# Sixteen experts in fourteen units: experts ordered by token count on the chip, shared units in column groups, four homes for weights

## What is computed

```
def moe_ffn(h, w_router, b_router, w1, w3, w2):
    s = sigmoid(h @ w_router); sb = s + b_router          # 16 experts in 4 groups
    gsel = argmax over groups of the sum of the group's top two sb
    idx = the two best experts inside that group; wsel = s[idx] / sum(s[idx])
    hid = silu(h @ w1[e]) * (h @ w3[e])                   # 1024 -> 256, for the chosen e
    return sum over the two chosen e of wsel * (hid @ w2[e])   # 256 -> 1024
```

## Time and profile before

| | us |
|---|---|
| median of 3 runs | 1189.07 (1189.02 to 1189.97) |
| the profiled execution's own time | 1190.82 |
| its span, first to last instruction | 1189.2 |
| PE busy | 1121.5 (94%) |
| DVE busy | 536.3 (45%) |
| ACT busy | 282.8 (24%) |
| POOL busy | 208.8 (18%) |
| mean granted TensorE clock | 0.992 |

### The profile page before, as it was taken

The page is one execution under the profiler, slowest core; times in us unless marked ns, Lnnn a source line. Parts: engine busy times, 40 slices in busy tenths (PEclk is TensorE's granted clock), DMA queues, the critical chain, the costliest instruction groups (busy, mean ns, idle before and its releaser), DMA issues.

```text
span 1189.2 us, 13631 instructions
## 1 busy us (share of the span) xinstructions
PE 1121.5 (94%) x4356; PEld 604.3 (51%) x4356; DVE 536.3 (45%) x1275; ACT 282.8 (24%) x653; POOL 208.8 (18%) x288
## 2 busy tenths in 40 slices
PE   5999999998999999999799999989899879999995
PEld 3556766554444454444355676745544435444442
DVE  1146543874237433433441545477623644333326
ACT  2121222663011211111141112156601111111111
POOL 5026101010115100000463410000112230000022
PEclk9999999999999999999999999999999999999998
DMA  9577822893207899998865941178300589999954
GB/s 350 209 245 289 315 109 92 349 370 145 107 26 279 323 386 366 368 367 302 322 231 154 388 149 36 43 293 337 107 18 0 189 343 354 359 373 371 358 176 196
DMA packets 63318, 291.17 MB, mean 245 GB/s; under 512 B 9504, under 2 KB 10672, under 8 KB 47328
## 3 DMA queue, kind: packets, MB, share of 16 engines
q1 hardware_dynamic: 33344, 190.87, 42.8%
q0 software_dynamic: 22720, 78.75, 18.6%
q10 hardware_dynamic: 7200, 20.87, 4.4%
HBM read 240.06 MB, written 56.98 MB: 250 GB/s over the span
## 4 chain that ended last, share of the span: by engine, by line
PE 84%; DVE 6%; DMA 4%; issue 2%; ACT 2%; POOL 1%; SPq 0%; ACTq 0%; POOLq 0%; DVEq 0%
PE ps L1235 13%; PE ps L1536 12%; PE ps L1715 9%; PE ps L1693 9%; PE ps L1696 9%; PE ps L1170 3%; PE ps L1163 3%; PE ps L1470 2%; PE ps L1501 2%; PE ps L1481 2%; PE ps L1146 2%; PE ps L1749 2%; DMA expert_in<-arena,pos_i 2%; PE ps L1145 2%; PE ps L1101 2%
## 5 line engine op out<-in xcount | busy, mean ns | idle before, releaser
L1235 PE MATMUL ps<-arena 128*128 128x320 f32 x560 | 156.6, 432 | 0.0
L1536 PE MATMUL ps<-arena 128*128 128x512 f32 x320 | 140.4, 594 | 2.4 <-issue 2.4
L1235 PEld LDWEIGHTS ps<-arena 128*128 128x128 f32 x560 | 105.0, 190 | 42.6 <-issue 1.0
L1715 PE MATMUL ps<-arena 128*128 128x512 f32 x256 | 115.4, 594 | 3.7 <-issue 3.7
L1693 PE MATMUL ps<-arena 128*128 128x512 f32 x256 | 117.2, 601 | 1.3 <-DVE arena L2791 1.3
L1696 PE MATMUL ps<-arena 128*128 128x512 f32 x256 | 115.1, 592 | 0.0
L2791 DVE COPY arena<-ps 128x512 f32<-128x512 f32 x32 | 22.1, 691 | 203.3 <-PE ps L1676 203.3
L1536 PEld LDWEIGHTS ps<-arena 128*128 128x128 f32 x320 | 59.5, 190 | 74.6 <-issue 74.6
L1693 PEld LDWEIGHTS ps<-arena 128*128 128x128 f32 x256 | 48.9, 192 | 62.5 <-issue 60.4
L1696 PEld LDWEIGHTS ps<-arena 128*128 128x128 f32 x256 | 48.6, 190 | 61.2 <-issue 61.2
L1715 PEld LDWEIGHTS ps<-arena 128*128 128x128 f32 x256 | 46.1, 190 | 50.5 <-issue 50.5
(11 more groups left out here) (332 smaller groups left out, 1652.2 us busy)
## 6 DMA issues: line engine op xcount, KB each, us to landing
arena<-in_w SPq DMA_DIRECT2D x96, 1024.0 KB, 9.3
arena<-in_w_ada SPq DMA_DIRECT2D x40, 1024.0 KB, 6.8
expert_in<-arena POOLq DMA_DIRECT2D x2, 8192.0 KB, 33.4
expert_out<-arena ACTq DMA_DIRECT2D x30, 512.0 KB, 8.1
arena<-expert_in POOLq DMA_DIRECT2D x28, 512.0 KB, 9.7
arena<-in_w_t SPq DMA_DIRECT2D x10, 1024.0 KB, 10.6
arena<-in_w_ada_c SPq DMA_DIRECT2D x8, 1024.0 KB, 13.2
arena<-in_w_out SPq DMA_DIRECT2D x8, 1024.0 KB, 6.1
```

The costliest lines, as they stand in the source:

```text
L1235: ins = mm(out[:, 0:HALF], lhs[:, k, :], rhs[:, k, :], start=(first and k == 0), stop=(last and k == 3), skip_group_check=True)
L1536: ins = mm(out[:, n * 512:(n + 1) * 512], yT[:, k, t * P:(t + 1) * P], w[k // 2][:, k % 2, n * 512:(n + 1) * 512], start=(k == 0), stop=(k ...
L1715: ins = mm(out[:, n * 512:(n + 1) * 512], hidT[:, f, :], w[:, f, n * 512:(n + 1) * 512], start=(f == 0), stop=(f == 1))
```

## The change

Nothing before the router changes. After the counts of tokens per expert are known, DVE orders experts 2 to 15 by count (larger count first) with pairwise comparisons of 14 by 14 and gives each a role: roles 2 to 9 are the eight with the fewest tokens ("low"), roles 10 to 15 the others; experts 0 and 1 keep roles 0 and 1. `roles_i` holds the expert of each role; each engine that needs it reads it with `value_load`. A low role has room for 96 rows a round, the others for 128. If more than six of the fourteen have over 96 rows, two rounds are run.

Four low roles share three units: each unit takes 96 rows of one role and 32 rows of the fourth. Two full units, six shared ones and six full ones make fourteen. In a shared unit every matmul is written as four, each over 32 columns of the token block, which land in 32 rows of the output; three use one expert's weights, one the other's. The loops over units are written out instead of hardware loops. There are four homes for weights; the two new ones lie where h2 was, so they are free only after the scatter. The slot rows in `expert_out` are numbered by role. An extra transfer of 1 MB of zeros at the beginning fills the 32 rows of low roles that no store writes.

```diff
+LOW_CAP = 96
+LOW_ROLES = 8
+def expert_units():
+    units = [[(0, 0, P, 0)], [(1, 0, P, 0)]]
+    for low in (2, 6):
+        units += [[(low + i, 0, LOW_CAP, 0), (low + 3, LOW_CAP, P - LOW_CAP, (P - LOW_CAP) * i)] for i in range(3)]
+    return units + [[(role, 0, P, 0)] for role in range(LAST_LOW, NE)]
+PLACE_OF = {0: 0, 1: 1, 2: 2, 5: 3, 3: 0, 4: 1, 6: 2, 9: 0, 7: 1, 8: 3, 10: 2, 11: 1, 12: 3, 13: 2, 14: 0, 15: 1}
+LOAD_ORDER = list(PLACE_OF)
+WEIGHTS_ORDER = sorted([(load, role) for role in LOAD_ORDER[2:-2] for load in ("up", "down")],
+                       key=lambda x: 2 * FIRST_UNIT[x[1]] + 3 * (x[0] == "down"))
...
+        up_at = [at_ring + SLOT, at_ring + 3 * SLOT, at_h + 2 * SLOT, at_h]
+        down_at = [at_ring, at_ring + 5 * SLOT, at_h + 4 * SLOT, at_up]
...
# SP
-                    load_up(2, 0, 0)
...
+                    wait(sp, roles_ready.sem, roles_ready.at(l, 1))
+                    filled(sp, l, "tokens0")
+                    wait(sp, scattered.sem, scattered.at(l, 16 * 2 * TT))
...
+                        for load, role in WEIGHTS_ORDER:
+                            e = sp.value_load(roles_i[0:1, role:role + 1], min_val=0, max_val=NE - 1)
+                            free = used_by(base, role)
+                            (load_up if load == "up" else load_down)(e, PLACE_OF[role], base + 2 if free is None else free)
...
# POOL
+                    pool.dma_start(y_d.rearrange("(e p) d -> p e d", p=P)[LOW_CAP:P, FIRST_LOW:LAST_LOW],
+                                   zeros[LOW_CAP:P, :].unsqueeze(1).broadcast_to((P - LOW_CAP, LOW_ROLES, D))).then_inc(spare_zeroed, 16)
...
+                        def load(u):
+                            b = u % 2
+                            wait(pool, hs_in[b], turn * of_round(ROWS_IN, b) + before_unit(ROWS_IN, u))
+                            wait(pool, hsT_full, base + u + 1)
+                            for role, lo, n, skipped in EXPERT_UNITS[u]:
+                                e = pool.value_load(roles_i[0:1, role:role + 1], min_val=0, max_val=NE - 1)
+                                src = slots_in(e, r) if n == P else some_slots_in(e, r, skipped, n)
+                                pool.dma_start(hs[lo:lo + n, b, :], src).then_inc(hs_in[b], 16)
...
# PE
+                def columns_of_unit(u):
+                    parts = EXPERT_UNITS[u]
+                    if len(parts) == 1:
+                        return [(0, P, parts[0][0])]
+                    return [(lo + i, 32, role) for role, lo, n, _ in parts for i in range(0, n, 32)]
...
+                    for k in range(KD):
+                        if k == 4:
+                            pe.wait_ge(hsT_high, base + u + 1)
+                        for lo, n, role in columns_of_unit(u):
+                            ins = mm(out[lo:lo + n, :], hsT[b][:, k, lo:lo + n], w[role][:, k, :], start=(k == 0), stop=(k == KD - 1),
+                                     skip_group_check=True)
...
-                        with pe.Fori(0, NE // 2 - 1) as i:
-                            for b in range(2):
-                                hidden(base, 2 * i + b, b)
-                                tokens(base, 2 * i + 2 + b, b)
-                                down(base, 2 * i + b, b)
-                                up(base, 2 * i + 2 + b, b)
+                        for u in range(UN - 2):
+                            hidden(base, u, u % 2)
+                            tokens(base, turn, u + 2)
+                            down(base, turn, u)
+                            up(base, turn, u + 2)
...
# ACT
-                    act.dma_start(slots_out(e), ys[:, b, :]).then_inc(ys_out[b], 16)
+                    for role, lo, n, skipped in EXPERT_UNITS[e]:
+                        act.dma_start(y_d[role * P + skipped:role * P + skipped + n, :], ys[lo:lo + n, b, :]).then_inc(ys_out[b], 16)
...
# DVE, between the line that sets rounds_i and modulation_rows
+                dve.tensor_scalar(r_over, total, float(LOW_CAP), None, ALU.is_gt)
+                dve.scalar_tensor_tensor(out=r_key, in0=total, scalar=float(NE), in1=count16, op0=ALU.mult, op1=ALU.add)
...
+                dve.tensor_scalar(rounds_i[:, 0:1], r_n[:, 5:6], r_n[:, 7:8], 1.0, ALU.max, ALU.add).then_inc(routed.sem, 1)
...
+                dve.tensor_copy(r_up[:, 0:2], count16[:, 0:2])
+                link(V(r_pair, per_column(keys), per_row(keys), ALU.is_ge))
+                link(dve.tensor_reduce(r_up[:, 2:NE], r_pair, AX.X, ALU.add))
+                dve.tensor_scalar(r_role_row, r_up, -float(P), float(NE * P), ALU.mult, ALU.add)
+                dve.tensor_scalar(r_cap_of, r_up, NE - LAST_LOW + 0.5, float(P - LOW_CAP), ALU.is_lt, ALU.mult)
+                link(V(r_pair, per_column(r_up[:, 2:NE]), per_row(names), ALU.is_equal))
+                link(V(r_pair, r_pair, per_column(names), ALU.mult))
+                link(dve.tensor_reduce(r_over[:, 2:NE], r_pair, AX.X, ALU.add))
+                dve.tensor_scalar(roles_i[:, 2:NE], r_over[:, 2:NE], -1.0, float(NE), ALU.mult, ALU.add).then_inc(roles_ready.sem, 1)
+                link(dve.tensor_scalar(r_cap_of, r_cap_of, float(LOW_CAP), None, ALU.add))
+                link(dve.memset(r_cap_of[:, 0:2], float(P)))
+                for of_expert, of_choice in ((r_role_row, r_role), (r_cap_of, r_cap)):
+                    link(V(r_t, r_sel, of_expert.unsqueeze(1).unsqueeze(1).broadcast_to((P, 2, TT, NE)), ALU.mult))
+                    link(dve.tensor_reduce(of_choice, r_t, AX.X, ALU.add))
```

More of the change, by code:

```diff
@@ L1052, in rounds @@
                                 .then_inc(gate2_in, 16)
-                        with pool.Fori(0, NE // 2 - 2) as i:
-                            load(2 * i + 4, 0)
-                            load(2 * i + 5, 1)
-                        wait(pool, ys_out[0], base * 8 + NE * 8)
-                        wait(pool, ys_out[1], base * 7 + NE * 7)
+                        for u in range(4, UN):
+                            load(u)
+                        for b in range(2):
+                            wait(pool, ys_out[b], turn * of_round(ROWS_OUT, b) + of_round(ROWS_OUT, b))
                         wait(pool, back_ready, pool.snap(turns, min_val=0, max_val=10) + 1)
@@ L1714, in down @@
                         for f in range(2):
-                            ins = mm(out[:, n * 512:(n + 1) * 512], hidT[:, f, :], w[:, f, n * 512:(n + 1) * 512],
-                                     start=(f == 0), stop=(f == 1))
+                            for lo, rows_of, role in columns_of_unit(u):
+                                ins = mm(out[lo:lo + rows_of, n * 512:(n + 1) * 512], hidT[:, f, lo:lo + rows_of],
+                                         w[role][:, f, n * 512:(n + 1) * 512], start=(f == 0), stop=(f == 1), skip_group_check=True)
                     ins.then_inc(dn_full, 1)
@@ L2786, in _ @@
                     gates_of_choices()
+                link(dve.scalar_tensor_tensor(out=r_gate2, in0=r_role, scalar=float((NE - 1) * P), in1=gates,
+                                              op0=ALU.is_equal, op1=ALU.mult))
+                link(V(r_gate, r_gate2[:, 0], r_gate2[:, 1], ALU.add))
                 def tokens(base, e, b):
@@ L2822, in rows_of_round @@
-                    dve.wait_ge(back_chain, turn * 9 + 3)
+                    role = r_role.rearrange("p a t -> p (a t)")
+                    cap = r_cap.rearrange("p a t -> p (a t)")
+                    V(r_in, r_rel, cap, ALU.is_lt).then_inc(back_chain, 1)
+                    V(r_at_row, role, r_rel, ALU.add).then_inc(back_chain, 1)
+                    dve.tensor_scalar(r_last, r_rel2, 1.0, None, ALU.add).then_inc(back_chain, 1)
+                    dve.wait_ge(back_chain, turn * 10 + 3)
@@ L2854, in rounds @@
                         hidden(base, 0, 0)
-                        with dve.Fori(0, NE // 2 - 1) as i:
-                            step(2 * i + 1, 1)
-                            step(2 * i + 2, 0)
-                        hidden(base, NE - 1, 1)
-                        output(base, NE - 2, 0)
-                        output(base, NE - 1, 1)
+                        for u in range(1, UN - 1):
+                            step(u, u % 2)
+                        hidden(base, UN - 1, 1)
+                        output(base, turn, UN - 2, 0)
+                        output(base, turn, UN - 1, 1)
                         dve.wait_ge(gate2_in, turn * 32 + 32)
```

265 lines of the change are left out of this document (156 added, 109 removed).

## The result

The changed kernel takes 1183.54 us (median of 6 runs) against 1189.82 for the kernel before beside it (6 runs): ratio 0.9943, 95% interval 0.9919 to 0.9966. That is 6.3 us gained where 27.3 were forecast, and it lies outside the range of 1150 to 1179. One of the six executions of the changed kernel ran in a slower state (1310.92 us at a mean clock of 0.844); the ratio leaves it out, and the median of the other five is 1182.16. The profiled execution took 1180.08 us, the shortest of the six, with a span of 1177.2. Lines L1235, L1536, L1594, L1652, L1676, L1693/L1696, L1715 and L1725 of before are now L1319, L1620, L1678, L1736, L1761, L1797, L1821 and L1831; the weight loads are L847 and L860, the row loads L1131.

The account below looks back on a forecast made before the run. PE was taken to bound the kernel, with DMA only some 7% behind. 45.6 - 5.2 - 3.6 - 9.5 = 27.3 us gained, so 1189.1 - 27.3 = 1161.8 us, range 1150 to 1179.

Parts of the forecast that it names:

- Two units less, and the excursions: Two units fewer per layer save 45.6 us of PE work; eight matmul shape excursions per layer cost 5.2 us.
- rival (e): Matmul groups with different weights do not run side by side; 0.09 us on each quad eats all the gain; chance 0.04.
- The ordering chain: Ordering experts on DVE before the expert loops takes 4.3 us; later loop starts cost 3.6 us over both layers.
- the zero transfer: 1 MB on POOL's queue ahead of layer 0's bias tables; 2.7 us if nothing hides it, left out of the sum.
- The ledger: Byte count of loads and stores in the expert stages at 395 GB/s, giving 9.5 us of waits in both layers.
- transfers at 395 GB/s: DMA rate taken for the expert stages, the mean of saturated windows at 416 and 377 GB/s.
- rival (b): Contention holds DMA at 368 GB/s in the expert stages; 24 us of waits, 1176 us; chance 0.15.
- PE's waits for weights: Waits before `up(2)` and `up(5)`: 2.5 and 2.0 us in layer 0, 3.0 and 2.0 in layer 1, together 9.5.
- clock drops "set off": Clock drops likely at `up(2)`, 1.8 us in each layer, offset by one already paid and by shorter second waits.
- (c): DMA ceiling below demand, 358 GB/s; last weight load 16.2 us late in each layer, 1185 us; chance 0.05.

Follow-up runs that it names:

- the kernel before with the zeros: The kernel before plus only the 1 MB transfer of zeros on POOL's queue: 1194.49 us, ratio 1.0051.
- late zeros: The changed kernel with the zeros written later, from DRAM to DRAM beside the work of the projections: 1178.37 us, ratio 0.9910.
- strided, late zeros: The changed kernel with zeros written later and shared units' rows in four 32-row loads to every fourth partition: 1163.53 us, ratio 0.9769.
- little traffic: The changed kernel with zeros written later, one row load per shared unit, half of w1 and w3 for roles 3, 4, 6 to 15: 1152.21 us, ratio 0.9679.
- the other order on DVE: The changed kernel with `modulation_rows` ahead of expert ordering in layer 0, and a `tokens0` copy ahead of its last part in layer 1: 1183.85 us, ratio 0.9966.
- the strided kernel: The changed kernel with shared units' rows in four loads of 32, load g to partitions g, g+4, and so on: 1166.08 us, ratio 0.9822.
- in blocks: The changed kernel with shared units' rows in four loads of 32, each to adjacent partitions: 1188.16 us, ratio 0.9998.

## Why the prediction was wrong, point by point

Where the time went shows best at fixed places of PE: the first matmul of L1652 (entry, layer 0) and of L1725 behind each layer's last unit, starts in us of the profiled executions, with the difference to before. Each row is a single execution: that of the changed kernel is its shortest, 10.7 us below that of before, where the medians differ by 6.3. And the kernel before with the zeros is 4.5 and 4.3 us late at the first two places and 0.7 early at the third, though its median is 6.2 us slower. So differences of some 5 us in a row can be chance. The forecast's steps for layer 0 are 22.8 - 2.6 - 2.1 - 4.5 = 13.6, for layer 1 22.8 - 2.6 - 1.45 - 5.0 = 13.7.

| | entry L1652 | L1725, layer 0 | L1725, layer 1 |
|---|---|---|---|
| before | 384.53 | 571.32 | 1145.96 |
| changed | 396.62 (+12.1) | 568.63 (-2.7) | 1133.68 (-12.3) |
| late zeros | 387.44 (+2.9) | 569.18 (-2.1) | 1133.22 (-12.7) |
| strided, late zeros | 390.27 (+5.7) | 556.84 (-14.5) | 1117.84 (-28.1) |
| little traffic | 389.87 (+5.3) | 554.53 (-16.8) | 1107.26 (-38.7) |
| forecast | +3.3 | -13.6 | -27.3 |

**Two units less, and the excursions: right.** Full 11.39, shared 11.68; the quads cost nothing beyond the excursion (rival (e) was wrong). Eight times 0.29 per layer stand where 0.33 was priced.

**The ordering chain: right.** 4.2 us against 4.3. With late zeros and nothing else the entry moved by 2.9 us, where 3.3 were forecast, and PE waited for `modulation_rows`, as forecast. The last two versions of the table moved by 5.7 and 5.3: in their executions, as in that of the changed kernel, PE waited 3.2 us for "remote" ahead of the chain and then ran at a lower clock (0.63 from 384 to 388 with little traffic). Five of the eleven profiles of the changed kernel and its versions have this wait, six don't; what it is stays open.

**Step that failed, 1: the zero transfer, "that is its cost if nothing hides it", 2.7 us, and taken to be hidden.** By itself it costs 6.2 us, and moving it gave back 4 to 5. The ledger priced the bytes, not the queue. The bias tables behind the zeros land 4 us later. Attention needs them much later, as the forecast said, but POOL waits for them at 78 us, and behind that wait stand the inverse roots on which PE depends. And the stall is paid twice, in idle time and in the lower clock behind it (0.52 for 7 us in the changed kernel, 0.76 in the kernel before with the zeros; the earlier trace rows had shown such a drop).

**Step that failed, 2: transfers at 395 GB/s wherever they queue.** The windows gave 371 and 358, the second under rival (b)'s 368. They are means of two levels: 414 to 420 without a split row load, 298 to 327 with one. The window of 377 from which 395 was averaged was no evidence for either. The forecast listed the split loads only by their issues and their bytes and never asked which partitions they write. With the step of four and late zeros the 12 us windows from 424 to 532 have 414 to 421, and PE's waits for weights, forecast at 9.5 us, are 6.8.

That the changed kernel's waits for weights add up to 9.6 us, just what was forecast (3.97 before `up(2)` of layer 1, 1.10 and 4.17 before the two `up(5)`), is luck: late entry and rows that land late (3.59) hid the rest, as the late zeros and the other order on DVE brought out with 18.5 and 20.9.

**Step that failed, 3: clock drops "set off".** The mean granted clock of the whole span tells their size: (1 - 0.978) x 1177.2 = 26 us of missing full clock against (1 - 0.992) x 1189.2 = 9.5 before, though part of it lies in idle stretches. In the repaired version it is 15, so even there the term is up to 6 us and not nothing.

```profile
core 0: 1177.2 us, clock 0.978
```

```profile
core 0: 1162.2 us, clock 0.987
```

The waits brought the drops with them: behind the 3.97 us before it, `up(2)` of layer 1 took 9.70 us instead of some 7.05:

```profile
985.81 9.70 PE L1797 MATMUL ps<-arena 128*32 128x512 f32 x64 [3.97 <-DMA arena<-in_w]
```

**The rivals.** What happened lies between (b) and (c) in time, but its mechanism, a row load whose layout slows all transfers, was none of them. The Trainium skill (DMA: Bandwidth & Descriptors, "Where 436 GB/s comes from") puts the limit between HBM and SBUF at about 358 GB/s, which would have given 1185, near the result. The trace disagrees, with one core running: 418 over 72 us, and the strided kernel 409 and 418; a nearly right number by a rule that does not hold here.

A rule that did bear on it was not weighed. The Trainium skill (SBUF — State Buffer, "Door 1: The DMA port swizzle (why `[64,N]` ≈ `[32,N]`)") says that what counts is how many of 16 ports a transfer's partitions reach: 32 adjacent ones reach eight, and in 0 to 95 eight ports have twice the partitions of the other eight. By that map each load with a step of four reaches all sixteen evenly. The trace agrees as far as it goes (312 to 324 in blocks, 416 to 425 strided). That such a load also slows the weights beside it, and that 96 partitions, which by the map reach all sixteen ports, do as badly as 32 (304 and 296), are findings of these runs. That the ports are the reason is not shown: which engine writes which partition no row here tells.

What stays open: row loads of 128 partitions run at 414 in the changed kernel and at 348 to 374 in the kernel before, at a share near 1 in both. In the latter the demand was no more than 368, but why the share is then not lower was not tried.

## What to carry to other kernels

Price a transfer by three things: its bytes, what stands behind it in its queue and who waits for that, and the partitions it writes. On this kernel splitting one load into parts of the partitions slowed all transfers beside it, and a layout with a step cost nothing on PE. A resource with 7% of slack hides a defect that takes the gain once a change uses up that slack. When a wait is removed and the time stays, look for the same time in the next wait before calling the wait harmless.

## What the runs showed of the hardware

- Row loads of 96 or 32 adjacent partitions take the core's transfers together from 414-426 to 296-328 GB/s while they run, at the same busy share of the engines (1.02 at 298 and at 415); the weights' packets beside them fall from 26.0 to 18.3 GB/s an engine.
- Four loads of 32 rows, each laid over partitions g, g+4, ..., run at 415 to 425, as well as one load of 128 rows (414 to 426).
- 1 MB put ahead of other transfers in one queue made those behind it land 4 us later (14.7 to 18.7 us after their issue, 11.8 to 14.4 without it).
- Reading the 32 columns of a matmul's stationary side with a step of four cost nothing: 11.68 us a unit either way.
- Reads and writes together kept 418 GB/s for 72 us on one core.
